# One expert stage of a fused two-layer block: paired 512-column operands, per-tile sums on VectorE between the steps of the routing

## What is computed

```
def peer(xn, peer_w_q, peer_sub_keys, peer_u, peer_v):
    qh = (xt @ peer_w_q).reshape(T, PEER_HEADS, 2, PEER_HALF)          # 8 heads, 2 halves of 128
    sub = jnp.einsum("thpc,hpnc->thpn", qh, peer_sub_keys)             # 128 sub-keys a half
    v1, i1 = lax.top_k(sub[:, :, 0], 16)
    v2, i2 = lax.top_k(sub[:, :, 1], 16)
    cand = (v1[..., :, None] + v2[..., None, :]).reshape(T, PEER_HEADS, 256)
    vals, cidx = lax.top_k(cand, 16)
    e1 = jnp.take_along_axis(i1, cidx // 16, axis=-1)
    e2 = jnp.take_along_axis(i2, cidx % 16, axis=-1)
    experts = e1 * 128 + e2
    gates = jax.nn.softmax(vals, axis=-1)
    ...
        h = jnp.einsum("cd,chkd->chk", xc, u_sel)
        a = jax.nn.gelu(h, approximate=False) * gc
        return jnp.einsum("chk,chkd->cd", a, v_sel)
```

## Time and profile before

| | |
|---|---|
| median of three runs | 3241.83 us |
| the profiled execution | 3241.25 us |
| its span, first to last instruction | 3239.4 us |
| TensorE busy | 98% of the span |
| GpSimd / VectorE / ScalarE busy | 77% / 50% / 46% |
| `u0` on TensorE | 1752.97 to 1937.36 us |

### The profile page before, as it was taken

How to read it: one execution, slowest core, us unless ns; L and a number is a source line. 1 busy time by engine, 2 the same in 40 slices (tenths; PEclk the granted TensorE clock), 3 DMA queues, 4 the chain that set the end, 5 groups by cost and what they waited for, 6 DMA issues and landing times.

```text
span 3239.4 us, 62053 instructions
## 1 busy us (share of the span) xinstructions
PE 3166.6 (98%) x22442; PEld 2805.2 (87%) x22442; DVE 1628.5 (50%) x2999; ACT 1484.7 (46%) x1981; POOL 2497.6 (77%) x1117
## 2 busy tenths in 40 slices
PE   8999889999999999998999999999999999999999
PEld 7888878988888888997789998888888888888888
DVE  3268646522222422497565958876612664157600
ACT  5466543544444444545454554443444334433433
POOL 6821245888888888888587887898898889887887
PEclk9999999999999999999999999999999999999999
DMA  6554203555555555653355555555555555555555
GB/s 223 185 167 127 84 18 124 193 190 188 188 189 191 184 190 190 200 163 124 111 184 170 183 182 174 173 182 177 173 196 187 177 179 183 189 182 172 176 193 168
DMA packets 158761, 553.20 MB, mean 171 GB/s; under 512 B 18000, under 2 KB 24288, under 8 KB 158496
## 3 DMA queue, kind: packets, MB, share of 16 engines
q1 hardware_dynamic: 152208, 541.37, 51.8%
q0 software_dynamic: 3248, 6.77, 0.9%
q10 hardware_dynamic: 3168, 3.15, 0.3%
HBM read 548.33 MB, written 2.88 MB: 170 GB/s over the span
## 4 chain that ended last, share of the span: by engine, by line
PE 67%; POOL 15%; issue 10%; DVE 5%; ACT 2%; DMA 1%; POOLq 0%; ACTq 0%; DVEq 0%; SPq 0%
PE ps L767 37%; PE ps L769 19%; POOL wl L604 15%; PE ps L755 6%; PE ps L1010 2%; DVE wl L1885 1%; PE ps L1320 1%; DVE arena L1964 0%; DMA xT<-x 0%; PE ps L834 0%; DMA raw<-w_z 0%; ACT wh L1428 0%; ACT under_u L1585 0%; PE ps L1041 0%; PE ps L951 0%
## 5 line engine op out<-in xcount | busy, mean ns | idle before, releaser
L604 POOL TENSOR_TENSOR wl<-raw,wh 128x1024 fp32r<-128x1024 f32 x980 | 2364.9, 2422 | 485.2 <-ACT wh L1428 483.0
L1428 ACT ACTIVATE wh<-raw 128x1024 fp32r<-128x1024 f32 (+1 forms) x1034 | 1084.3, 1053 | 1415.9 <-PE ps L769 1185.0
L767 PE MATMUL ps<-uhl,wh 128*128 128x512 f32 x3200 | 1120.0, 395 | 11.6 <-DVE uhl L1867 11.3
L769 PE MATMUL ps<-uhl,wl 128*128 128x256 f32 x3200 | 891.5, 279 | 0.0
L767 PEld LDWEIGHTS ps<-uhl,wh 128*128 128x128 f32 x3200 | 601.5, 188 | 150.1 <-DVE wl L1885 10.1
L769 PEld LDWEIGHTS ps<-uhl,wl 128*128 128x128 f32 x3200 | 604.0, 189 | 0.1
L755 PE MATMUL ps<-uhl,wh 128*128 128x256 f32 x2976 | 548.6, 287 | 3.6 <-POOL wl L604 1.2
L767 PE MATMUL ps<-ehl,wh 128*128 128x512 f32 x1536 | 551.6, 400 | 0.4 <-POOL wl L604 0.4
L755 PEld LDWEIGHTS ps<-uhl,wh 128*128 128x128 f32 x2976 | 468.4, 193 | 11.2 <-issue 6.3
L1876 DVE TENSOR_REDUCE ps<-ps 128x256 f32<-128x512 f32 x168 | 117.3, 698 | 634.6 <-PE ps L769 633.8
L769 PE MATMUL ps<-ehl,wl 128*128 128x256 f32 x1536 | 431.7, 281 | 0.0
(11 more groups left out here) (365 smaller groups left out, 3620.0 us busy)
## 6 DMA issues: line engine op xcount, KB each, us to landing
raw<-w_u SPq DMA_DIRECT2D x256, 512.0 KB, 3.6
raw<-w_v SPq DMA_DIRECT2D x256, 512.0 KB, 3.5
raw<-w_gu SPq DMA_DIRECT2D x176, 512.0 KB, 3.6
raw<-w_down SPq DMA_DIRECT2D x80, 512.0 KB, 3.7
raw<-w_out SPq DMA_DIRECT2D x64, 512.0 KB, 4.0
raw<-w_z SPq DMA_DIRECT2D x54, 512.0 KB, 4.1
raw<-w_in SPq DMA_DIRECT2D x52, 512.0 KB, 4.1
raw<-w_qkv SPq DMA_DIRECT2D x48, 512.0 KB, 3.7
```

Source lines behind the costliest of these rows:

```text
L604: pool.tensor_tensor(wl[:, slot, 0:width], raw[:, slot, 0:width], wh[:, slot, 0:width].bitcast(F32), ALU.subtract).then_inc(lo_ready, 1)
L767: pe.matmul(bank(b).rearrange("p (n t) -> p n t", n=2), wh[:, slot, at], both, start=first and c == 0, stop=False, skip_group_check=True)
L769: ins = pe.matmul(bank(b)[:, 0:T], wl[:, slot, at], high, start=False, stop=last and c == kt - 1, skip_group_check=True)
L1428: act.activation(wh[:, slot, 0:width], raw[:, slot, 0:width], ACT.Copy).then_inc(hi_ready, 1)
```

## The change

`u0` is multiplied with `pair_unit`, its four tiles of a turn into banks 4 to 7. VectorE adds the halves of each tile into one of two places in PSUM (`EARLY_SUMS`, banks 0 and 1), and ScalarE takes its gelu from there. `SUMS_FROM` goes, since now all `u` stages count their sums in `exp_sum`.

These 32 sums have to be done by VectorE while it does the routing. They are put between the routing's steps by a small planner that runs when the kernel is built: `sums_between(us)` adds an assumed duration to a clock and places the next sum as soon as the clock has passed 5.55 us times the tile's number plus 1. Two sums (tiles 30 and 31) stand behind the softmax's last step, the other thirty before it.

The picks are made for eight heads at once: instead of 48 instructions of 256 elements for each half of the tokens, six of 2048 elements, through a bigger `pick` in the arena. `topf` and `it16` move to banks 2 and 3.

ScalarE takes the gelu of a tile one tile later than before, behind the conversions that the next tile releases; for the last tile that is behind the last conversions of the stage. The exponentials stand behind the gelu of tile 29.

TensorE's waits: at the start of `u0` tile j waits for the j-th of the first four copies of the sub-key scores (`sub_ev`); later tile m waits for the sum of tile m - 4. At the start of `u1` the wait is as before, for the gelus of tiles 30 and 31 (`u_ev`), whose sums now lie in the two banks that `u1` writes first.

```diff
-SUMS_FROM = 1
...
-        pick = view(misc, 8 * T, 2, TOPK, TOPK)
+        pick = view(arena, 2 * DT * T, PH, TOPK, TOPK)
...
+        EARLY_SUMS = [ps[:, b:b + 1, 0:T] for b in range(2)]
-        topf = ps[:, 6, :].rearrange("p (t n k) -> p t n k", t=2, n=2 * PH)
-        it16 = ps[:, 7, 0:TOPK]
+        topf = ps[:, 2, :].rearrange("p (t n k) -> p t n k", t=2, n=2 * PH)
+        it16 = ps[:, 3, 0:TOPK]
...
-                    if first and q == 0 and j < 2:
+                    if first and q == 0:
                         pe.wait_ge(sub_ev, j + 1)
+                    elif q == 0:
+                        pe.wait_ge(exp_sum, i * 4 + (j - 3))
                     elif first and q == 1 and j < 2:
                         pe.wait_ge(u_ev, QJ + j - 1)
...
-                        if q == 0:
-                            ins = unit(bank(4 + j % 2)[:, 0:T], ready, g % RING,
-                                       lambda c: uh[:, UKT * n + c, :], lambda c: ul[:, UKT * n + c, :],
-                                       first=n == 0, last=n == 1)
-                        else:
-                            ins = pair_unit(j % 2, ready, g % RING, UHL, UKT * n, first=n == 0, last=n == 1)
+                        ins = pair_unit(4 + j if q == 0 else j % 2, ready, g % RING, UHL, UKT * n, first=n == 0,
+                                        last=n == 1)
...
+            def first_gelu(n, k):
+                act.wait_ge(exp_sum, n + (k + 1))
+                act.activation(HB[0][:, bass.ds(n + k, 1), :], EARLY_SUMS[k % 2], ACT.Gelu).then_inc(u_ev, 1)
+
+            def first_gelus(i, start=False):
+                for j in range(4):
+                    ahead(BASE["u0"] + 2 * j, i, 8)
+                    if j or not start:
+                        first_gelu(i * 4, j - 1)
...
-            with act.Fori(0, 7) as i:
-                gelus(0, i)
-            act.wait_ge(soft_in, 2)
-            for t in range(2):
-                act.activation(val[:, t, :, :], val[:, t, :, :], ACT.Exp).then_inc(soft_ex, 1)
-            gelus(0, 7)
+            first_gelus(0, start=True)
+            with act.Fori(1, 7) as i:
+                first_gelus(i)
+            for j in range(4):
+                ahead(BASE["u0"] + 2 * j, 7, 8)
+                first_gelu(28, j - 1)
+                if j == 2:
+                    act.wait_ge(soft_in, 2)
+                    for t in range(2):
+                        act.activation(val[:, t, :, :], val[:, t, :, :], ACT.Exp).then_inc(soft_ex, 1)
+            first_gelu(28, 3)
...
+            TILE_US, TOP_US, PAIR_US, PICK_US, SUM_US = 5.55, 1.5, 3.2, 6.6, 0.75
+            at_us, summed = [1.5], [0]
+
+            def sum_next():
+                n = summed[0]
+                dve.wait_ge(w_used, BASE["u0"] + 2 * n + 2)
+                if n >= 2:
+                    dve.wait_ge(u_ev, n - 1)
+                else:
+                    dve.wait_ge(sub_ev, 8)
+                add_halves(EARLY_SUMS[n % 2].rearrange("p a t -> p (a t)"), 4 + n % 4).then_inc(exp_sum, 1)
+                summed[0] += 1
+
+            def sums_between(us):
+                at_us[0] += us
+                while summed[0] < QJ - 2 and at_us[0] >= TILE_US * (summed[0] + 1) + 1.0:
+                    sum_next()
+                    at_us[0] += SUM_US
...
                 for n in range(2 * PH):
                     top16(SUB[:, t, n, :], top[:, t, n, :], topi[:, t, n, :].bitcast(U32), wk[:, n % 2, 0:NK])
+                    sums_between(TOP_US)
...
                     top16(c, val[:, t, h, :], vali[:, t, 0, h, :].bitcast(U32), wk[:, h % 2, :])
+                    sums_between(PAIR_US)
...
-                for h in range(PH):
-                    for n in range(2):
-                        p1 = pick[:, n, :, :]
-                        link(dve.tensor_tensor(p1, valf[:, t, n, h, :].unsqueeze(2).to_broadcast([P, TOPK, TOPK]),
-                                               it16.unsqueeze(1).to_broadcast([P, TOPK, TOPK]), ALU.is_equal))
-                        link(dve.tensor_tensor(p1, p1, topf[:, t, 2 * h + n, :].unsqueeze(1)
-                                               .to_broadcast([P, TOPK, TOPK]), ALU.mult))
-                        link(dve.tensor_reduce(exs[:, t, n, h * TOPK:(h + 1) * TOPK], p1, AX, ALU.add))
+                for n in range(2):
+                    four = [P, PH, TOPK, TOPK]
+                    link(dve.tensor_tensor(pick, valf[:, t, n, :, :].unsqueeze(3).to_broadcast(four),
+                                           it16.unsqueeze(1).unsqueeze(1).to_broadcast(four), ALU.is_equal))
+                    sums_between(PICK_US / 3)
+                    best = topf[:, t, :, :].rearrange("p (h e) k -> p e h k", e=2)[:, n]
+                    link(dve.tensor_tensor(pick, pick, best.unsqueeze(2).to_broadcast(four), ALU.mult))
+                    sums_between(PICK_US / 3)
+                    link(dve.tensor_reduce(exs[:, t, n, :].rearrange("p (h k) -> p h k", h=PH), pick, AX, ALU.add))
+                    sums_between(PICK_US / 3)
...
+            while summed[0] < QJ - 2:
+                sum_next()
             for t in range(2):
                 dve.wait_ge(soft_ex, t + 1)
...
+            while summed[0] < QJ:
+                sum_next()
             dve.wait_ge(et_ps, 1)
```

More of the change, by code:

```diff
@@ L1349, in experts_in @@
                     else:
-                        pe.wait_ge(*((u_ev, i * (4 * span) + (QJ * q + 4 * k + j - 1)) if q < SUMS_FROM else
-                                     (exp_sum, i * (4 * span) + (QJ * (q - SUMS_FROM) + 4 * k + j - 1))))
+                        pe.wait_ge(exp_sum, i * (4 * span) + (QJ * q + 4 * k + j - 1))
                     for n in range(2):
@@ L1370, in experts_out @@
                     elif first and q < NQ - 1:
-                        pe.wait_ge(exp_sum, QJ * (q + 2 - SUMS_FROM) + d - 1)
+                        pe.wait_ge(exp_sum, QJ * (q + 2) + d - 1)
                     else:
@@ L1783, in _ @@
                         .then_inc(sub_ev, 1)
-            def u_bank(q, j):
-                return 4 * (1 - q) + j % 2 if q < 2 else 4 + j
             def gelus(q, i, round_turn=None, rounds={}):
@@ L1795, in gelus @@
                     ahead(g, i, 8)
[L1796 to L1805, removed]
+                    act.wait_ge(exp_sum, i * 4 + (QJ * q + j + 1))
+                    tile = TILE_SUMS[j % 2].unsqueeze(1) if q == 1 else ps[:, 4 + j:5 + j, 0:T]
+                    act.activation(HB[q][:, bass.ds(i * 4 + j, 1), :], tile, ACT.Gelu).then_inc(u_ev, 1)
+            def first_gelu(n, k):
[6 more added lines that the diff above has]
+                        first_gelu(i * 4, j - 1)
             def round_experts(q, k):
@@ L2412, in top16 @@
                 link(dve.max_index(index[:, 8:16], best[:, 8:16], work))
+            TILE_US, TOP_US, PAIR_US, PICK_US, SUM_US = 5.55, 1.5, 3.2, 6.6, 0.75
[14 more added lines that the diff above has]
+                    at_us[0] += SUM_US
             dve.wait_ge(sub_ev, 4)
-            link(dve.tensor_copy(it16, cst("iota")[:, 0:TOPK]))
             for t in range(2):
@@ L2419, in _ @@
                     top16(SUB[:, t, n, :], top[:, t, n, :], topi[:, t, n, :].bitcast(U32), wk[:, n % 2, 0:NK])
+                    sums_between(TOP_US)
+                if t == 0:
+                    dve.wait_ge(sub_ev, 8)
+                    link(dve.tensor_copy(it16, cst("iota")[:, 0:TOPK]))
                 link(dve.tensor_copy(topf[:, t, :, :], topi[:, t, :, :].bitcast(U32)))
```

## The result

The changed kernel took a median of 3248.93 us over 20 runs (3240.94 to 3259.98), the kernel before 3241.66 us over 20 (3239.21 to 3248.25). The ratio is 1.0020, with a 95% interval of 1.0014 to 1.0026: slower by some 6.5 us. Forecast were 3237.5 us, faster by 0.13%, and a range up to 3246. The profiled execution after was the longest of its 20, 3259.98 us with a span of 3258.2, 18.8 us more than the span before, so what follows compares stages and not spans.

A forecast was written before the change was run, and what follows sets the result against it. TensorE was taken to bound `u0`, without stalls. From 3241.25 us, 6.8 gained in its units and 2.4 lost at its end gave 3236.9, or 3237.5 as a median; forecast 3235 to 3239, wider range 3231.5 to 3246.

The forecast's parts named there:

- The unit: Matmuls of `u0`: a unit takes 2.773 us instead of 2.879, so 64 units gain 6.8 us; lower bound 3.4.
- Behind TensorE: Conversions and splits in `u0`: a slot needs 3.9 us, TensorE returns after 8.3; slack 4.4 us, price nothing.
- the 11.6 from which TensorE was to stall: Sums in `u0`: TensorE stalls when a sum starts more than 7.2 + 4.4 = 11.6 us behind its tile.
- VectorE's load: Routing during `u0`: picks fall from 43.8 to 27.6 us; with 26 sums the routing takes 151.9 us instead of 149.1.
- Are the sums in time?: Sums in `u0`: at most 6.6 us behind their tile, at the 19th, which costs nothing.
- the cover of 5.0 us: Sums in `u0`: the margin left between the greatest forecast lateness, 6.6 us, and a TensorE stall at 11.6.
- The end of `u0`: Between `u0` and `u1`: softmax and tile 30's gelu add a stall of 2.4 us, bounds 1.6 to 5.
- The sum: Whole kernel: 3241.25 - 6.8 + 2.4 = 3236.9 us profiled; median 0.6 higher, 3237.5 us, 0.13% less.
- signs of being wrong: Profile after: splits 2.83 or 2.88 us apart, long ScalarE waits for sums in `u0`, or another pace in untouched stages.
- Rival 2: Routing in `u0`: VectorE becomes the bound, wide picks held to 5.9 us instead of 2.27; 3259 us, chance 0.09.

The follow-up runs named there:

- 3: The changed kernel without the 32 sums of `u0`, gelu taken from the first half of the bank alone: ratio 0.9990 to the kernel before, 3240.23 us.
- 5: The changed kernel with outer sums' second operand in PSUM, exponentials one tile earlier and tile 30's gelu before the last conversion: 0.9978, 3237.26 us.
- 2: The changed kernel with the planner's costs set to durations without holds (1.75, 2.9, 7.0 us): ratio 1.0049 to the kernel before, 3259.38 us.
- 6: The changed kernel with the planner paying for holds (1.75, 3.9 and 7.4 us): ratio 1.0007 to the kernel before.
- 1: The changed kernel with the second operand of the 16 outer sums copied to PSUM: ratio 0.9987 to the kernel before, 3240.84 us.
- 7: The kernel before with one idle VectorE instruction (0.7 us) behind each of the 16 routing heads: ratio 1.0066.
- 4: The changed kernel with exponentials after tile 28's gelu and tile 30's gelu ahead of the last conversion: ratio 1.0015 to the kernel before, 3248.98 us.

## Why the prediction was wrong

- *The unit* was right: 2.773 us forecast and 2.77 found; 177.46 us from the first to the last matmul of `u0` in 3 and 5.
- *Behind TensorE* was right: room of 4.4 us. The 11th sum was 13.5 us late, 1.9 more than the 11.6 from which TensorE was to stall, and the first stall was 1.9 us (a start 2.0 us behind the one in front, where 0.12 is usual). In 2 it was 12.7 us late and the stall 1.1 us; in 6 no sum was over 11.2 and there was none.
- *VectorE's load* was right for picks and sums and **wrong for the routing's own steps**. This is the step that failed: I took 149.1 us less picks for what the rest costs, as if the duration of an instruction belonged to it and stayed when sums are put in between. The outer sums were 8.0 us there and 21.5 after (+13.5), the casts, shifts and a copy behind the heads another 6. So the sums ran not 6.6 but up to 16.3 us behind.
- *Are the sums in time?* inherited it: the cover of 5.0 us was overrun by a term that I had not looked for. Where the outer sums are free of holds (1) the 19th sum was 7.3 us behind, forecast 6.6, and the latest, the 24th, 8.4, inside the cover.
- *The end of `u0`* was right: the forecast had 2.4 us of new stall, and 3.18 - 0.69 = 2.5 were found in the change and in 1 and 3, in all three with the exponentials, the last conversion and the table load as counted. The load ran ahead of its sum: it began at 1948.61 and the sum was done at 1949.2. The drain that the Trainium skill, ScalarE: Activation LUTs, section "What ACT_TABLE_LOAD costs", adds to a switch is not in these traces: the gelu starts at 1949.90, 1.29 us after the load.
- *The sum* holds for the kernel that I had costed, one without holds: it had 4.4 us less from first to first, and 1 gave 4.3 less and a ratio of 0.9987, the forecast one.
- Two of the signs of being wrong came true: ScalarE waited 74.7 us for sums inside the stage, and in the profile after untouched stages had another pace (`u2` 2.83 us a unit instead of 2.77). The second is not the cause, by 1 and 5, where `u2` ran at 2.83 too and the kernel was faster.
- *Rival 2* had the mechanism, the point (5 us beyond the count) and the direction, and the wrong instruction (and so its 3259 was not reached). I weighed it on the picks, whose operand in PSUM frees them, and did not ask which of the routing's steps have both in SBUF. The rule was there: the Trainium skill, GPSIMD Engine Reference, section "8. Key points", says that GpSimd shares its SBUF interfaces with VectorE and that instructions with two SBUF inputs contend. The traces agree (up to 2.5 us with two in the change, 0.41 to 0.42 with one in PSUM in 1).
- Accounting of the change: 188.1 us from first to last matmul in `u0` against 177.5 in 5, 10.6 more. By the distance between the ends of units, about 7.9 are in six units with a wait, 1.7 in the dip at 1858 and 1.0 in the 19 units behind the waits that took 2.82 or 2.83 instead of 2.77 us. The last two were not separated by an experiment.

## What to carry to other kernels

A short duration in a trace may be a matter of step: an instruction that contends with another engine looks free as long as it meets the end of that engine's instructions or a gap between them, and anything put between two of them changes its price. So before placing work between existing steps, list which of them contend with a busy neighbour, and cost those at up to the length of the neighbour's instruction (here 2.6 us instead of 0.42). And where one engine works through a queue for two others (here ScalarE, with gelus for VectorE and conversions for TensorE), write down how late an input may be before the second is starved; that number, 11.6 us, held to a tenth or two in the change and in 2.

## What the runs showed of the hardware

- Held instructions can fall into step with the engine that holds them: in 7 they took 2.62 us each, exactly two splits apart; in the change, out of step, anything from 0.42 to 2.53. GpSimd is held as well, by less: in 3, where outer sums began just before a split, that split took up to 2.61 us instead of 2.41. Instructions with a single input in SBUF were held as well: a cast of 256 elements took 0.29 us before and 2.39 once in the change, a shift of 128 elements 0.23 and 2.33.
- The pace of pairs isn't a property of the code. The first stage is the same in all ten kernels; its units took mostly 2.82 or 2.83 us in nine profiles and 2.77 in one. `u2` took 2.77 in five and 2.83 in the other five, `v3` 2.80 in eight and 2.77 in two. In the change the pace went from 2.77 to 2.83 within `u0`, behind its waits. What sets it wasn't tried. A stage of 64 units moves by 3.4 us with it, which may be part of why runs of one kernel spread over 10 us and more; that was not shown.
- The granted clock fell to half behind waits of TensorE of 2.0 us (4, at 1854 us) to 23 us (7), but not each time: the same 3.18 us at the end was followed by a dip in the change and in 2, and by none in 1 and 3.
